# Prompt-key rows loaded during the delta stage, and the sample's state updates placed one to a level

## Time and profile before

| | us |
|---|---|
| median of 3 runs | 2986.49 (2976.23 to 2989.47) |
| the profiled execution | 2982.73 |
| its span, from the first to the last instruction | 2981.1 |
| PE busy | 2711.8 (91%) |
| DVE busy | 1076.6 (36%) |
| ACT busy | 679.6 (23%) |
| POOL busy | 526.2 (18%) |
| mean granted PE clock, as a share of 2.4 GHz | 0.948 |

### The profile page before, as it was taken

The page is one execution under the profiler, slowest core; times in us unless marked ns, Lnnn a source line. Parts: engine busy times, 40 slices in busy tenths (PEclk is TensorE's granted clock), DMA queues, the critical chain, the costliest instruction groups (busy, mean ns, idle before and its releaser), DMA issues.

```text
span 2981.1 us, 35497 instructions
## 1 busy us (share of the span) xinstructions
PE 2711.8 (91%) x13308; PEld 1714.3 (58%) x13308; DVE 1076.6 (36%) x2419; ACT 679.6 (23%) x1235; POOL 526.2 (18%) x528
## 2 busy tenths in 40 slices
PE   8999996897678995887799987999999999999999
PEld 5555556797434442554456555666666666666665
DVE  3565644664356541344210113104443333330000
ACT  2443321232255662333210003111000000000000
POOL 0110012343144433332030010011010010100000
PEclk9999997898689997999899998999999999999999
DMA  5101114102110118776441111721111111122220
GB/s 204 40 31 47 47 40 160 42 23 68 37 25 21 35 53 280 243 250 230 173 147 68 64 57 59 211 73 44 42 29 42 28 42 28 42 25 69 69 69 15
DMA packets 212112, 243.70 MB, mean 82 GB/s; under 512 B 57281, under 2 KB 156098, under 8 KB 211586
## 3 DMA queue, kind: packets, MB, share of 16 engines
q1 hardware_dynamic: 190034, 163.70, 18.2%
q0 software_dynamic: 20112, 73.54, 6.9%
q10 hardware_dynamic: 1824, 4.57, 0.4%
HBM read 208.15 MB, written 37.81 MB: 83 GB/s over the span
## 4 chain that ended last, share of the span: by engine, by line
PE 48%; issue 1%; ACT 1%; DVE 1%; DMA 0%; POOL 0%; DVEq 0%; POOLq 0%; ACTq 0%
PE tr_acc L3125 22%; PE tr_acc L2970 12%; PE tr_acc L3165 11%; PE tr_acc L2951 1%; PE tr_m L3031 1%; PE tr_acc L3008 1%; ACT tr_small L3256 1%; PE tr_m L3058 0%; DMA ahead_main<-in_w_xv 0%; PE tr_acc L3040 0%; POOL tr_f L2914 0%; PE tr_m L2979 0%; DVE tr_small L3383 0%; DVE tr_mx L3373 0%; PE tr_m L2988 0%
## 5 line engine op out<-in xcount | busy, mean ns | idle before, releaser
L3125 PE MATMUL tr_acc<-tr_hnT,ahead_main 128*128 128x364 f32 (+1 forms) x2112 | 644.0, 468 | 0.0
L3125 PEld LDWEIGHTS tr_acc<-tr_hnT,ahead_main 128*128 128x128 f32 x2112 | 401.2, 190 | 242.1
L1094 PE MATMUL front_wide<-front_w_nat,front_x 128*128 128x512 f32 (+1 forms) x576 | 224.2, 546 | 0.0
L1094 PEld LDWEIGHTS front_wide<-front_w_nat,front_x 128*128 128x128 f32 x576 | 109.4, 190 | 107.5 <-issue 95.7
L3165 PE MATMUL tr_acc<-tr_early,ahead_main 128*128 128x364 f32 (+1 forms) x528 | 161.5, 468 | 0.0
L3165 PE MATMUL tr_acc<-tr_early,tr_hnT 128*128 128x364 f32 (+1 forms) x528 | 161.5, 468 | 0.0
L3491 DVE TENSOR_TENSOR tr_small<-tr_acc,tr_rbc 128x728 f32<-128x728 f32 x44 | 40.3, 917 | 335.5 <-PE tr_acc L3125 335.5
L2931 POOL TENSOR_TENSOR tr_early<-tr_small 128x1088 f32 x22 | 54.7, 2484 | 591.7 <-ACT tr_small L3312 591.7
L3312 ACT ACTIVATE tr_small<-tr_small 128x1088 f32<-128x1088 f32 x22 | 24.4, 1110 | 581.5 <-DVEq L3508 581.5
L1080 PE MATMUL front_acc<-front_x,front_w_c 128*128 128x364 f32 (+1 forms) x480 | 149.2, 470 | 0.0
L3165 PEld LDWEIGHTS tr_acc<-tr_early,ahead_main 128*128 128x128 f32 x528 | 100.3, 190 | 60.6
(11 more groups left out here) (495 smaller groups left out, 3851.0 us busy)
## 6 DMA issues: line engine op xcount, KB each, us to landing
ahead_main<-in_cache_kv SPq DMA_DIRECT2D x136, 256.0 KB, 4.4
ahead_main<-in_w_up SPq DMA_DIRECT2D x44, 512.0 KB, 5.0
ahead_main<-in_cache_kv POOLq DMA_DIRECT2D x80, 256.0 KB, 4.7
ns_last<-in_cache_kv POOLq DMA_DIRECT2D x40, 256.0 KB, 4.9
tr_early<-in_cache_memT POOLq DMA_DIRECT2D x2, 4096.0 KB, 15.7
ahead_main<-in_cache_memV POOLq DMA_DIRECT2D x2, 4096.0 KB, 14.5
front_w_c<-in_w_chan SPq DMA_DIRECT2D x12, 512.0 KB
front_w_nat<-in_w_nat POOLq DMA_DIRECT2D x3, 2048.0 KB, 15.4
```

The source lines that it names most:

```text
L1094: mm = pe.matmul(wide[:, s, 0:b - a], x[:, k, i * P:(i + 1) * P], w_nat[:, k, a:b], start=(k == 0), stop=(k == KD - 1))
L3125: mm = pe.matmul(acc[a][:, g, 0:hi - lo], w_up[:, n, a, k, :], hnT[:, k, lo:hi], start=(k == 0), stop=(k == KD - 1))
```

## The change

`ss` is no longer a tile of the delta stage. `Keys` has a buffer `room` of 4096 numbers per partition, which holds the states in the delta stage and the prompt keys' rows (`rows`, 3072, and `wk`, 1024) afterwards; the size is that of both. When the four stores of the states have landed, SP issues the eight loads of rows inside the delta stage, after tile 3's output store and tile 5's `zt` load; the prompt keys' stage has them no more.

The updates are moved as well: half 0 stays in level 4, one product `sample_kv` stands at each place on PE, and on DVE update 1 is in level 4, 2 and 3 in level 5, 4 behind `scores_out(a)`, 5 behind `scores_out(b)`, and 6 and 7 behind the first takes of pair 1. `finish(SAMPLE)` now comes behind `scores_out(b)`.

```diff
@@ -96,7 +96,7 @@
         gc = st.sb("gc", [P, 36])
         ex = st.sb("ex", [P, 3, 36])
         S = st.sb("S", [P, H, P])
-        ss = st.sb("ss", [P, H, NB, P])
+        ss = keys.states()
         vx = st.sb("vx", [SAMP, 2, NB, P])
         bsel = st.sb("bsel", [SAMP, NB])
         back = st.sb("back", [P, H, 2, SAMP])
@@ -283,6 +283,12 @@
                     sp.dma_start(scr["mix"][cols(t), 512:1024], flat(o[s])).then_inc(o_out[s], 16)
                     if t + 2 < 2 * PAIRS:
                         sp.dma_start(flat(zt[s]), scr["z"][cols(t + 2), :]).then_inc(z_here[s], 16)
+                    if t == 3:
+                        sp.wait_ge(state_out, 64)
+                        for n in range(4):
+                            r, two = slice(2 * n * P, 2 * (n + 1) * P), slice(2 * n, 2 * n + 2)
+                            sp.dma_start(keys.rows()[:, two, :], io["rows"][r, 0:384].rearrange("(t p) n -> p t n", p=P)).then_inc(keys.rows_here[n], 16)
+                            sp.dma_start(keys.win_keys()[:, two, :], io["wrows"][r, 0:P].rearrange("(t p) n -> p t n", p=P)).then_inc(keys.rows_here[n], 16)
                 sp.wait_ge(S_ready, 2 * PAIRS)
                 sp.dma_start(io["gstate_p"].rearrange("h k d -> k h d"), S[:, :, :]).then_inc(state_out, 16)
                 sp.wait_ge(state_out, 80)
@@ -485,14 +491,12 @@
                         if l == 4:
                             if p == 0:
                                 sample_kv(1)
-                                sample_kv(2)
                         if l == 5 and p == 0:
-                            sample_kv(4)
-                            sample_kv(5)
+                            sample_kv(3)
                         if l == 6:
                             query_pairs(a)
                             if p == 0:
-                                sample_kv(7)
+                                sample_kv(5)
                         zx_products(a, l)
                         zx_products(b, l)
                         if p and l == 3:
@@ -518,14 +522,18 @@
                             if more:
                                 decay_rows(d)
                             if p == 0:
-                                sample_kv(3)
+                                sample_kv(2)
                         if l == 5:
                             if more:
                                 key_pairs(d)
                             if p == 0:
-                                sample_kv(6)
+                                sample_kv(4)
                     query_pairs(b)
+                    if p == 0:
+                        sample_kv(6)
                     solve(a)
+                    if p == 0:
+                        sample_kv(7)
                     solve(b)
                 for t in (6, 7):
                     state_products(t)
@@ -854,6 +862,9 @@
                     more = p < PAIRS - 1
                     take_z(a, 0)
                     take_z(b, 0)
+                    if p == 1:
+                        sample_state(6)
+                        sample_state(7)
                     if p > 1:
                         new_values(a - 2)
                     for l in range(1, 6):
@@ -892,28 +903,27 @@
                                 spread(1)
                         if l == 4:
                             keys_out(b)
+                            if p == 0:
+                                sample_state(1)
+                                spread(2)
                             if more:
                                 arguments(d)
+                        if l == 5:
                             if p == 0:
-                                sample_state(1)
                                 sample_state(2)
-                                spread(2)
                                 sample_state(3)
                                 spread(3)
-                        if l == 5:
                             if more:
                                 matrix(d)
-                            if p == 0:
-                                sample_state(4)
-                                sample_state(5)
-                                sample_state(6)
-                            else:
+                            if p:
                                 finish(b - 2)
                     scores_out(a)
                     if p == 0:
-                        sample_state(7)
+                        sample_state(4)
+                    scores_out(b)
+                    if p == 0:
+                        sample_state(5)
                         finish(SAMPLE)
-                    scores_out(b)
                 for t in (6, 7):
                     new_values(t)
                     new_state(t)
@@ -1285,8 +1295,19 @@
 
     def __init__(self, nc, ctx):
         self.wblk = ctx.enter_context(nc.sbuf_tensor("keys_wblk", [P, 2, 32, P], F32, side="right"))
+        self.room = ctx.enter_context(nc.sbuf_tensor("keys_room", [P, 4096], F32, side="right"))
         self.w_here = nc.alloc_semaphore("keys_w_here")
+        self.rows_here = [nc.alloc_semaphore(f"keys_rows_here{n}") for n in range(4)]
         self.copied = nc.alloc_semaphore("keys_copied")
+
+    def states(self):
+        return self.room[:, :].rearrange("p (h b n) -> p h b n", h=4, b=NB)
+
+    def rows(self):
+        return self.room[:, 0:3072].rearrange("p (t n) -> p t n", t=SEQ // P)
+
+    def win_keys(self):
+        return self.room[:, 3072:4096].rearrange("p (t n) -> p t n", t=SEQ // P)
 
 
 def stage_channels_and_delta(nc, io, scr, ident, half, ctx):
@@ -1306,14 +1327,12 @@
     wblk = keys.wblk
     with Stage(nc, "pk") as st:
         pe_in = st.sb("pe_in", [P, 2, 32])
-        rows = st.sb("rows", [P, NK, 384])
-        wk = st.sb("wk", [P, NK, P])
+        rows, wk, here = keys.rows(), keys.win_keys(), keys.rows_here
         cT = st.sb("cT", [P, 2, 16, NC])
         vraw = st.sb("vraw", [P, P])
         turned = [st.ps(f"turned{s}") for s in range(2)]
         acc = [st.ps(f"acc{s}") for s in range(2)]
         wide = st.ps("wide")
-        here = [st.sem(f"here{n}") for n in range(4)]
         pe_here = st.sem("pe_here")
         v_here = st.sem("v_here")
         turn_done = st.sem("turn_done")
@@ -1326,10 +1345,6 @@
 
             @block.sync
             def _(sp):
-                for n in range(4):
-                    r = slice(2 * n * P, 2 * (n + 1) * P)
-                    sp.dma_start(rows[:, 2 * n:2 * n + 2, :], io["rows"][r, 0:384].rearrange("(t p) n -> p t n", p=P)).then_inc(here[n], 16)
-                    sp.dma_start(wk[:, 2 * n:2 * n + 2, :], io["wrows"][r, 0:P].rearrange("(t p) n -> p t n", p=P)).then_inc(here[n], 16)
                 sp.dma_start(pe_in[:, :, :], io["cmp_peT"]).then_inc(pe_here, 16)
                 sp.dma_start(vs[:, :, :], io["rows"][0:SEQ, 384:512].rearrange("(t p) n -> p t n", p=P)).then_inc(v_here, 16)
                 sp.dma_start(vw[:, 4:, :], io["wrows"][0:SEQ, 128:256].rearrange("(t p) n -> p t n", p=P)).then_inc(v_here, 16)
```

## The result

The changed kernel takes 2968.05 us (median of 8 runs, 2964.28 to 2970.42) against 2986.3 (8 runs, 2976.23 to 2991.41): a ratio of 0.994, 95% interval 0.9926 to 0.9955. That is 18.3 us (13.4 to 22.1 by the interval), where 20.4 were forecast. A second set of runs gave 0.9936 (0.9919 to 0.9953). The profiled execution took 2968.8, with a span of 2967.2.

A forecast was written before the change was run, and what follows sets the result against it. Pair 0 was taken as bounded by the order of DVE's work, then PE's clock, the keys' stage head by waiting for loads. Gains of 15.0 and 5.4 us, 20.4 together, off 2983.7 gave 2963, range 2952 to 2978.

The forecast's parts named there:

- State updates in pair 0: Delta stage, first pair of tiles: spreading the sample's updates gains 15.0 us, 6.2 from waits, the rest from PE's clock.
- the sample product: PE in pair 0 of the delta stage: each product on the sample's states costs 0.96 us.
- The stall: PE in pair 0, before `sample_kv(4)`: a wait of 0.9 us for DVE stays where 2.68 stood.
- Keys' stage: Head of the prompt keys' stage: PE no longer waits for rows, block products start at 740.55 instead of 745.97, gaining 5.4 us.
- Costed at nothing: Updates 6 and 7 in pair 1 hidden behind a DVE stall; SP's eight early loads covered by 22 us: 0 taken.
- The signs: Right: pair 0 near 61 us, clock close to 1.00; wrong: `skv_free` wait above 2 us or a stretch at 0.5.
- Rival 1: Pair 0: POOL's `tm` starts first and delays spread 2, the clock falls; gain 12.7 us, 2971; chance 0.18.
- Rival 2: Prompt keys' stage: early transposes lower PE's clock, block products run wholly at 0.50; gain 15.2 us, 2968.5; chance 0.13.
- Rival 3: Pair 0: PE's clock falls from 532.07 on and stays down; 5.7 us slower, 2989.4; chance 0.07.

The follow-up runs named there:

- 1 and 2: Each part alone against the kernel before: only the updates spread, 2974.49 us, ratio 0.9957; only the eight loads early, 2979.68 us, ratio 0.998.
- experiment 6: The change with dummy memsets and drains added on DVE: eight ahead of update 1, 2979.6 us; four ahead of update 2, 2979.08 us; one run each.
- experiment 5: The change with PE's places kept but DVE's updates and spreads in the order of before: 2973.55 us in one run.

## Why the prediction was right

*Direction, mechanism and most of the size.* 2968.05 against 2963, inside 2952 to 2978. Both gains are there in the places named, each without the other (1 and 2). Of the 5 us between forecast and result 2.6 are the base: the sum was taken off 2983.7, the mean of four executions, and eight runs of before have their median at 2986.3. Nearly all the rest is the gain, 18.3 for 20.4, a difference that the interval does not resolve.

*State updates in pair 0: 15.0 forecast, 14.3 between the two first profiles* (42.05 to 27.73); over the three profiles with the old order, 40.70 to 42.05, it is 13.0 to 14.3. The term that was mis-sized is the sample product. I took 0.96 from two of them in a row; one between groups of another kind costs 532.52 − 531.46 = 1.06, and there are seven from the first place on: 0.7 too little. The stall was 0.57, not 0.9, which gives 0.3 back; groups beside a product, which take 0.99 to the next start (554.27 to 555.26) for 0.89 elsewhere (558.30 to 559.19), cost some 0.3 more. The waits and the low clock went as said. The two traces give the split: 4.38 + 2.68 − 0.57 = 6.5 of waits, and 14.3 − 6.5 = 7.8 of clock, less what the new spacing costs. That the clock's part hangs on the gaps is what experiment 6 shows.

*Keys' stage: 5.4 forecast, 5.5 measured* (41.59 to 36.06). The forecast put the block products 9.10 behind the first transpose (740.55 − 731.45); it was 9.08. Over all profiles the stage has 40.0 to 41.6 with late loads, 33.9 to 36.1 with early ones; the spread is the clock during the turns and block products.

*Costed at nothing, and nothing:* updates 6 and 7 left the next take where it was, 564.77 − 559.19 = 5.58 behind the first transpose as before (579.70 − 574.12); SP had 18 us left behind the eight loads; pair 1 kept its 48.12.

*The signs.* Pair 0 was to take near 61 us at a clock close to 1.00; it took 63.39 at 0.95, and a stretch at 0.50, named as a sign of being wrong, is in it. But it lies in levels 1 and 2, ahead of the change, and the kernel before has one there too: 1.62 of the 2.3 us are lost there, which is no effect of the change (the kernel before takes 34.04 and 35.66 there in its two profiles), and 0.7 in the changed part.

*Rival 1, DVE against POOL:* the two did meet, in the order that costs nothing, and by a margin so small that this was partly luck. Spread 2 began 0.27 us ahead of POOL and kept its 1.22; POOL's `tm` took 2.08 for 1.26, off the path. That agrees with the rule of the Trainium skill cited there ("SBUF — State Buffer", "Who interferes with whom"): who starts first goes on. The sample's `finish`, free of POOL now, took 1.13 instead of 2.98.

*Rival 2, the clock at the block products:* it did not come; they took 8.68 us at 0.80, as before.

*Rival 3, the clock in pair 0:* it did not come either; the clock is 1.00 from `sample_kv(1)` on. Its cost was real, though: behind a wait of 0.57 or 1.35 us the clock stayed up (the change, experiment 5), but with one of 3.38 it went, and took back 10.4 of the 14.3.

*What I did not see:* the forecast treats everything outside the two stages as fixed. In the twelve profiles pair 0 up to level 4 takes 32.4 to 40.6 us and the attention 354.7 to 362.4, with nearly the same work. The profile of before had both near their short ends (34.04 and 355.58). That moved no term of the gain, but it made the profiled execution of before a short one: the two profiles differ by 13.9, the medians by 18.3.

## What to carry to other kernels

Where two engines hand work to and fro through two buffers, try one hand-over in each step of the main loop instead of two in a row: here moving the producer's places alone gave 13.5 of 14.3 us. A gap in PE's work can have two prices, the wait and the lower clock behind it; in experiment 6 the second was 3.1 and 3.7 times the first (12.3 by 4.0, 10.4 by 2.8), in the kernel before about 1.2 times (7.8 by 6.5). Loads at a stage's head can be hidden when SP can issue them in the stage before, into a tile that is already free: that gave 5.5 us in the keys' stage, while 4 us gained at the attention's head were not seen to reach the end. And two profiles of one kernel should be compared before a difference in a stage that nobody touched is explained.

## What the runs showed of the hardware

- Behind gaps of 3.38 and 4.56 us in pair 0, PE's clock stayed at 0.50 (1.2 GHz) for some 23 us or more in which PE was busy throughout; behind one of 4.38 us in the kernel before it was back after some 5 us; behind one of 1.35 us it stayed at 1.00.
- The clock in levels 1 and 2 of pair 0 falls in eleven of twelve profiles, for different lengths: in the same order of PE's instructions it was 1.00 throughout once (60.13 us) and 0.50 for at least 13.65 us the other time (68.28).
- Apart from the clock the trace repeats: the stretch from `sample_kv(1)` to pair 1 took 27.72 or 27.73 us in six profiles.
